# Projection: a block's three groups of turns spread between the chunks of the next block

## The reference, cut to what matters

```python
def in_projection(h, w_in):
    z = h @ w_in                                   # (1088, 1024) @ (1024, 2628)
    dq, dk, dv, sq, sk, sv, iq, ik, iw = jnp.split(z, cuts, axis=-1)
...
new_rows = (dk, dv, sk, sv, ik)                    # returned, row by token
...
score = einsum(wi, relu(qi . ki));  _, sel = lax.top_k(score, topk)
```

## Time and profile before

| | us |
|---|---|
| median of three runs | 1500.2 |
| the three runs | 1497.41 to 1500.4 |
| the profiled execution | 1499.62 |
| its span, first to last instruction | 1497.9 |
| TensorE busy in the span | 1421.3 (95%) |
| VectorE busy | 1065.1 (71%) |
| ScalarE busy | 645.0 (43%) |
| mean granted TensorE clock | 0.974 of full |

### The profile page before, as it was taken

The page is one execution under the profiler, slowest core; times in us unless marked ns, Lnnn a source line. Parts: engine busy times, 40 slices in busy tenths (PEclk is TensorE's granted clock), DMA queues, the critical chain, the costliest instruction groups (busy, mean ns, idle before and its releaser), DMA issues.

```text
span 1497.9 us, 26711 instructions
## 1 busy us (share of the span) xinstructions
PE 1421.3 (95%) x9519; PEld 1230.4 (82%) x9519; DVE 1065.1 (71%) x2317; ACT 645.0 (43%) x1362; POOL 323.0 (22%) x357
## 2 busy tenths in 40 slices
PE   5998999999789999989997999999999999999997
PEld 3775999899456666658887999999999999888876
DVE  4526999998789888783578666666566656875687
ACT  4546222222577776772564332233223332533353
POOL 3111111111111000030112543344334440000011
PEclk9999999999699999979999999999999999999999
DMA  9410456633555455532323323332333216995333
GB/s 298 126 50 17 133 178 202 204 111 99 113 157 153 145 137 136 117 113 78 115 83 100 97 89 114 86 104 80 114 114 111 73 58 227 307 322 190 115 89 141
DMA packets 180148, 198.28 MB, mean 132 GB/s; under 512 B 19757, under 2 KB 136814, under 8 KB 180058
## 3 DMA queue, kind: packets, MB, share of 16 engines
q1 hardware_dynamic: 180058, 197.11, 43.6%
HBM read 154.00 MB, written 43.08 MB: 132 GB/s over the span
## 4 chain that ended last, share of the span: by engine, by line
PE 86%; DVE 5%; ACT 3%; issue 2%; DMA 2%; SPq 1%; POOL 0%; DVEq 0%; POOLq 0%; ACTq 0%
PE PJ L2506 15%; PE S L2788 14%; PE S L2865 8%; PE T L2788 8%; PE PJ L2788 8%; PE S L2651 5%; PE PJ L2865 4%; PE T L2865 4%; PE S L2759 4%; PE T L2626 3%; PE PJ L2759 3%; PE PJ L2713 2%; PE PJ L2716 2%; PE S L2562 1%; PE S L2657 1%
## 5 line engine op out<-in xcount | busy, mean ns | idle before, releaser
L1794 DVE TENSOR_SCALAR_CACHE_REDUCE scrap<-work,cand 128x384 uint8<-128x384 f32 (+6 forms) x217 | 177.9, 884 | 1.1
L2506 PE MATMUL PJ<-hTh,wh 128*128 128x352 f32 (+2 forms) x480 | 160.7, 335 | 0.0
L2506 PE MATMUL PJ<-hTh,wl 128*128 128x352 f32 (+2 forms) x480 | 157.5, 328 | 0.0
L2506 PE MATMUL PJ<-hTl,wh 128*128 128x352 f32 (+2 forms) x480 | 157.4, 328 | 0.0
L662 POOL TENSOR_TENSOR wab_a<-graw,wab_a 128x512 fp32r<-128x512 f32 x63 | 87.4, 1401 | 247.0 <-ACT wab_a L1396 247.0
L1136 POOL TENSOR_TENSOR wl<-wraw,wh 128x1024 fp32r<-128x1024 f32 (+1 forms) x21 | 49.5, 2358 | 273.8 <-ACT wh L1230 273.8
L2098 DVE TENSOR_TENSOR mix_later<-mix_later,S 128x256 f32<-128x256 f32 (+1 forms) x147 | 60.9, 427 | 66.2 <-PE S L2788 65.2
L2788 PE MATMUL S<-tokA,wab_a 128*128 128x256 f32 x792 | 99.9, 285 | 0.2 <-ACT mix_later L1396 0.2
L2788 PEld LDWEIGHTS S<-tokA,wab_a 128*128 128x128 f32 x792 | 97.9, 193 | 0.6 <-issue 0.5
L2506 PEld LDWEIGHTS PJ<-hTh,wh 128*128 128x128 f32 (+1 forms) x480 | 90.6, 189 | 7.8 <-issue 6.4
L1396 ACT ACTIVATE aT<-T 128x512 f32<-128x512 f32 (+4 forms) x168 | 67.9, 452 | 56.2 <-PE T L2626 55.7
(11 more groups left out here) (360 smaller groups left out, 3581.6 us busy)
## 6 DMA issues: line engine op xcount, KB each, us to landing
graw<-in_w_gu SPq DMA_DIRECT2D x44, 512.0 KB, 5.4
ada<-in_w_ada SPq DMA_DIRECT2D x16, 1024.0 KB, 7.3
draw<-in_w_down SPq DMA_DIRECT2D x55, 256.0 KB, 3.6
h_scratch<-hid SPq DMA_DIRECT2D x22, 544.0 KB, 3.5
s_scratch<-hsum SPq DMA_DIRECT2D x11, 1024.0 KB, 4.2
draw<-s_scratch SPq DMA_DIRECT2D x44, 256.0 KB, 3.7
wraw<-in_w_in SPq DMA_DIRECT2D x20, 512.0 KB, 5.8
draw<-h_scratch SPq DMA_DIRECT2D x33, 256.0 KB, 3.0
```

The costliest lines, as they stand in the source:

```text
L1794: ins = nc.vector.tensor_scalar(scrap[0:r, o:o + n], work[0:r, o:o + n], least_score, None, ALU.is_ge, ALU.add, accum_out=rows_at(count, i))
L2506: last = pe.matmul(chunk_bank(3 * b + c)[0:w, 0:n], wp[:, b % 2, k, 0:w], hp[:, k, c0:c0 + n], start=(k == 0 and p == 0), stop=(k == KB - ...
```

## The change

Group c of natural block b - 1 is turned by TensorE right behind chunk c of block b, and emptied by ScalarE right behind the evacuation of that chunk. For the first natural block (block 1, behind block 2, where the cache turns use the banks) all three groups stay together. The list `T_ORDER` keeps its order. `nat_out` and the new `turn_block` do one group instead of three.

```diff
--- before.py
+++ after.py
@@ -115,6 +115,16 @@
 def ada_turn(j):
 
     return (j - ADA_FIRST) // 2 + 1, j - 2 if j >= ADA_FIRST + 2 else None
+
+
+def nat_groups(b, c):
+
+
+    if b - 1 not in NATURAL:
+        return []
+    if b - 1 == NATURAL[0]:
+        return [0, 1, 2] if c == 3 else []
+    return [c] if c < 3 else []
 
 
 LAST = NT - 1
@@ -1352,22 +1362,21 @@
                         last = nc.scalar.activation(ikD[dst, SEQ:SEQ + PAST], bank[0:64, 256:512], ACT.Copy)
                     last.then_inc(freed(("cache", j)), 1)
 
-            def nat_out(b):
+            def nat_out(b, q):
 
                 s = nat_slot[b]
                 w = BLOCKS[b][3]
-                for q in range(3):
-                    bank = t_wait_full(act, ("nat", b, q))
-                    if q == 0 and nat_count[b] > 0:
-                        act.wait_ge(nat_stored[s], 32 * nat_count[b])
-                    nt, r = (4, 128) if q < 2 else (1, DEC)
-                    view = bank[0:r, 0:128 * nt].rearrange("p (t e) -> p t e", e=128)
-                    e = 64 if BLOCKS[b][0] == "ik" else 128
-                    if BLOCKS[b][0] == "ik":
-                        nc.scalar.activation(iwn[0:r, 4 * q:4 * q + nt, :], view[:, :, 64:68], ACT.Copy,
-                                             scale=NH_I ** -0.5)
-                    nc.scalar.activation(nat[0:r, s, 4 * q:4 * q + nt, 0:e], view[:, :, 0:e], ACT.Copy
-                                         ).then_inc(freed(("nat", b, q)), 1)
+                bank = t_wait_full(act, ("nat", b, q))
+                if q == 0 and nat_count[b] > 0:
+                    act.wait_ge(nat_stored[s], 32 * nat_count[b])
+                nt, r = (4, 128) if q < 2 else (1, DEC)
+                view = bank[0:r, 0:128 * nt].rearrange("p (t e) -> p t e", e=128)
+                e = 64 if BLOCKS[b][0] == "ik" else 128
+                if BLOCKS[b][0] == "ik":
+                    nc.scalar.activation(iwn[0:r, 4 * q:4 * q + nt, :], view[:, :, 64:68], ACT.Copy,
+                                         scale=NH_I ** -0.5)
+                nc.scalar.activation(nat[0:r, s, 4 * q:4 * q + nt, 0:e], view[:, :, 0:e], ACT.Copy
+                                     ).then_inc(freed(("nat", b, q)), 1)
 
             for b in range(NB):
                 for c in range(4):
@@ -1384,8 +1393,8 @@
                         chunk_evac(b, c)
                     if c < 3 and b == 2:
                         cache_out(c)
-                if b - 1 in NATURAL:
-                    nat_out(b - 1)
+                    for q in nat_groups(b, c):
+                        nat_out(b - 1, q)
                 if b and b + 2 < NB:
                     split_w(b + 2)
                 for j in ada_after(b):
@@ -2580,6 +2589,16 @@
                         last = pe.transpose(bank[0:64, 128 * m:128 * m + 128], cachek[:, i, 640:704], ident[:, :])
                 last.then_inc(filled(("cache", j)), 1)
 
+            def turn_block(v, q):
+
+                wv = BLOCKS[v][3]
+                pe.wait_ge(chunk_out, 3 * (v + 1))
+                bank = t_wait_free(pe, ("nat", v, q))
+                for t in range(4 * q, min(4 * q + 4, NT)):
+                    o = 128 * (t - 4 * q)
+                    last = pe.transpose(bank[0:rows_of(t), o:o + wv], nat_source(v, t), ident[0:wv, 0:wv])
+                last.then_inc(filled(("nat", v, q)), 1)
+
             for b in range(NB):
                 kind, _, _, w = BLOCKS[b]
                 if b == 3:
@@ -2591,18 +2610,10 @@
                         chunk(b, c, dots_pairs(b, 2 * c + 1))
                     if c < 3 and b == 2:
                         turn_cache(c)
+                    for q in nat_groups(b, c):
+                        turn_block(b - 1, q)
                 for j in ada_after(b - 1)[1:]:
                     ada_transposes(j, j)
-                if b - 1 in NATURAL:
-                    v = b - 1
-                    wv = BLOCKS[v][3]
-                    pe.wait_ge(chunk_out, 3 * (v + 1))
-                    for q in range(3):
-                        bank = t_wait_free(pe, ("nat", v, q))
-                        for t in range(4 * q, min(4 * q + 4, NT)):
-                            o = 128 * (t - 4 * q)
-                            last = pe.transpose(bank[0:rows_of(t), o:o + wv], nat_source(v, t), ident[0:wv, 0:wv])
-                        last.then_inc(filled(("nat", v, q)), 1)
                 for j in ada_after(b):
                     if j == ADA_FIRST:
                         pe.wait_ge(relu_done, NH_I * len(TOPK_TILES))
```

## The result

The changed kernel takes 1505.34 us (median of 15 runs, 1500.46 to 1508.04) against 1499.81 us of the kernel before on the same chip (15 runs, 1495.9 to 1502.34): a ratio of 1.0035, 95% interval 1.0024 to 1.0046. I had forecast 1494.0 and faster. The projection did become shorter by more than I had said; the search on VectorE became longer by about eleven microseconds, and that was not in my sum as I had it.

The account below looks back on a forecast made before the run. TensorE was taken to set the projection's pace, with the turns on its path. Gains of 2.9 + 1.2 + 2.3 = 6.4 us there, 6.0 carried past the handover, gave 1494.0 us against 1500.2; range 1490.0 to 1497.6.

Parts of the forecast that it names:

- Moved past queues: ScalarE's earlier copies and SyncE's order cost nothing; VectorE's search starts 1.0 later, keeps its length, ends at about 370.6.
- Groups between chunks: A group of turns between two chunks costs TensorE 0.44 us, 0.88 per block for two groups.
- rival 2: Turn groups between chunks cost 0.70 each, as together; only block 4 gains, about 2 us: 1498; chance 0.09.
- Block 4: At its end, 4.20 us shrinks to 0.28 while its last chunk moves back 1.0: 2.9 us gained.
- Blocks 5 to 7: At each block's end, 1.57 - 0.28 - 0.88 = 0.41 us gained, 1.2 in all.
- Blocks with modulation products: Six blocks (8 to 11, 13, 15): end 3.15 instead of 4.42, 0.39 us gained each, 2.3 in all.
- The projection's end: The projection's last chunk comes 6.4 us earlier, its evacuation near 365.7.
- The handover: From projection to attention: tile 1's q lands at 383.0, VectorE's chain allows 6.0 us earlier; the later decides, 6.0.
- Rival 1: At the handover the search becomes the bound; only VectorE's 2.4 us arrive: about 1497.5; chance 0.12.
- Rival 4: TensorE's clock stays at half beyond 403, into tile 2; with four slow steps about 1504; chance 0.06.
- Rival 3: TensorE's full clock returns sooner, the dry stretch before tile 1's first scores closed: 3 us more, 1491; chance 0.13.
- The sign I had named: At the handover, tile 1's first scores beginning later than 386 would show the forecast wrong.

Follow-up runs that it names:

- experiment 2: The kernel before, with GpSimd's weight split waiting for chosen steps of VectorE's search, chosen by its own block ends: 1500.72 us, ratio 1.0006.
- experiment 4: The kernel before, with GpSimd's weight split of each block cut into eight instructions: 1499.6 us, ratio 0.9997.
- experiment 5: The kernel before, with GpSimd's weight split of every block done twice, writing the same values: 1521.25 us, ratio 1.0134.
- experiment 1: The changed kernel, with GpSimd's weight split from block 8 on waiting for a chosen search step, to lie beside counts alone (paced): 1493.27 us, ratio 0.9955.
- experiment 3: The changed kernel, with GpSimd's weight split of each block cut into eight instructions, without pacing: 1492.49 us, ratio 0.9952.
- experiment 6: The changed kernel, with turns spread only in blocks 4 to 7 and all three groups together from block 8 on: 1496.55 us, ratio 0.9985.

## Why the prediction was wrong, point by point

- **The step that failed** stands in "Moved past queues": "its length (to 369.46) is its own, so it ends at about 370.6 with the gates". The start was right to a tenth (141.7 forecast, 141.92 less 0.20 measured). The length was not its own: 228.8 us before already had 7.0 of holds by GpSimd, and with the new length of the blocks it has 17.8. I had followed the moved work past ScalarE's, SyncE's and TensorE's queues, but not GpSimd's, whose split moves with each block's end; and I had read VectorE's idle time ahead of the search but not the spread of its durations. The rows stood in the trace of before: updates of up to 1.601 and 2.23 us against a median of 0.167.
- **Groups between chunks:** 0.77 from product to product against the 0.76 I took. Right to within 0.1 (see blocks 5 to 7); rival 2, at 0.70 a group, falls.
- **Block 4:** its successor's first product at 142.35 instead of 145.12, 3.0 earlier without the offset, forecast 2.9; the last product pushed back by 1.0 without the offset, as forecast.
- **Blocks 5 to 7:** block 5's end is 0.20 where I had 0.28, but from first product to first product the block takes 13.01 (142.35 to 155.36) instead of 13.27 (145.12 to 158.39). That is 0.26 gained; blocks 6 and 7 gain 0.44 and 0.30. It is 1.0 in all instead of 1.2: with the end taken off, a group costs 0.46 to 0.55 us of the block's time, not 0.44. Where the 0.1 goes I didn't follow.
- **Blocks with modulation products:** block 9's end is 3.05 where I had 3.15. Block 10's first product is 4.7 earlier without the offset (212.41 against 216.87); the terms to there, 2.9 + 1.2 + 2 x 0.39, made 4.9. Behind it 3.2 more were gained where I had 1.6: 0.5 instead of 0.39 in each of blocks 10, 11, 13 and 15, and 1.1 in block 12, for which I had nothing. Block 12's gain is about TensorE's wait for its row copy, 1.0 by the view of waits before, for which I had expected no change and which is not among TensorE's waits after. It isn't all the change's: block 12 is 0.35 to 0.52 shorter also in experiments 2, 4 and 5, which leave the turns alone. The 0.1 of the others I didn't follow.
- **The projection's end:** 7.8 us earlier, forecast 6.4. The term was undersized, mostly by block 12.
- **The handover:** where the holds are out of the way (experiment 1), q lands at 382.39, forecast 383.0, and the time is 1493.27, forecast 1494.0. That the figures agree so closely is partly luck: the projection gained more than forecast, and the pacing makes the search 5 us shorter than the 228.8 that the sum carried. The fairer test is experiment 3, where the search is 227.3 long: tile 1's first scores come 6.8 earlier without the offset (forecast 6.0), and the time is 1492.49. One small term was too low: from the gates to the first bias of tile 0 it is 1.46 (381.57 to 383.03 in the changed kernel), where I had 1.0; TensorE's turn of the gates, an estimate of 0.5, shows as a wait of VectorE of 0.49. So that part of the sum held within 1 us; it only needed a search that ends in time.
- **Rival 1** named the right engine, "the search becomes the bound", but priced it as if the search could only start later: 1497.5. That it could become longer was not among its conditions, and so no case of mine was slower by way of the search.
- **Rival 4** has a share in it. The longer dry stretch keeps TensorE at half its clock until about 410; of the 7.2 us by which the span is longer, 5.4 are there at tile 1's first scores and 1.5 more are lost from these to tile 2's (437.95 - 395.06 = 42.9 against 41.4). But the clock came back within tile 1, and the dry stretch is made by the late gates. With the gates early (experiment 3) tile 1 takes 41.6 from its first scores to those of tile 2 (at 423.29), as before.
- **Rival 3** was not seen: with the gates early the clock is at half from 368 to past 392.
- **The sign I had named** as showing me wrong, tile 1's first scores later than 386, was the one that came: 395.06.

## What to carry to other kernels

Before calling the length of an engine's serial chain its own, look at the least, median and greatest duration of its small instructions: a median of 0.167 us with a greatest of 2.4 was here the sign that another engine holds it, and a look at what runs beside the long ones told which. Where a chain with a fixed step meets a block with a fixed length, a few tenths of a microsecond in either can turn chance meetings into one in every block, so shortening one engine can lengthen another. The cure here was cheap: cut the holding instruction into pieces, or place it beside instructions that it doesn't hold.

## What the runs showed of the hardware that I had not expected

- A VectorE update of 128x7 elements, 0.17 us, takes up to 2.40 us if it begins while GpSimd runs a tensor_tensor of 128x1024 elements (2.38 us); it ends with that instruction. Updates with two tensors as input and updates with one (`step<-step`, `good<-good`) are both held. The counts (a compare with an accumulated sum, 0.5 to 1.28 us) never were: 12 of them began beside the split in the changed kernel and 39 in the paced one, each as long as elsewhere.
- Two GpSimd memsets one after the other (0.73 and 0.78 us) held an update with one input, `step<-step`, for 1.49 us (experiment 6). So it isn't the subtraction alone that holds.
- Cut into eight, the same GpSimd work takes 3.38 us, and the longest update beside it 0.49.
- Only VectorE's side of the hold shows: from 150 on GpSimd's instruction stays at 2.37 to 2.43 us in the eight kernels that leave it whole, whether updates were held beside it or not. Where it begins just behind the start of an update (223.22 and 223.24 in experiment 5), the update takes its 0.17 and GpSimd 2.41.
